# First weight slab and x loaded and rounded in alternating halves, constants queued later, six projection pieces in banks of their own

## The reference

```python
def rms_norm(x, g):
    xf = x.astype(jnp.float32)
    y = xf * lax.rsqrt(jnp.mean(xf * xf, axis=-1, keepdims=True) + EPS) * g.astype(jnp.float32)
...
def parallel_mixer(h, w_in, ...):
    proj = h @ w_in
    qk_m, v_m, o_m, i_pre, f_pre, qkv_s = jnp.split(proj, PROJ_SPLITS, axis=-1)
    qk_m = jax.nn.silu(causal_depthwise_conv(qk_m, conv_w, conv_b))
...
x = x + parallel_mixer(rms_norm(x, mix_norm_g[l]), w_in[l], ...)
```

## Time and profile before

| what | value |
|---|---|
| median of 3 runs | 1740.88 us (1739.35 to 1741.17) |
| the profiled execution, its own time | 1739.95 us |
| its span in the profile | 1738.1 us |
| PE busy | 1566.5 us, 90% of the span |
| DVE busy | 1213.2 us, 70% |
| ACT busy | 850.8 us, 49% |
| POOL busy | 364.6 us, 21% |
| mean DMA rate | 242 GB/s |

### The profile page before, as it was taken

One profiled execution on the slowest core, in us unless ns is written; L12 is line 12 of the kernel. 1 busy time (PEld: TensorE's weight loads), 2 busy tenths in 40 slices (PEclk: granted clock), 3 DMA queues, 4 the chain that ended last, 5 costly groups with the idle time before them and its releaser, 6 DMA issues.

```text
span 1738.1 us, 23835 instructions
## 1 busy us (share of the span) xinstructions
PE 1566.5 (90%) x9202; PEld 1186.1 (68%) x9202; DVE 1213.2 (70%) x2403; ACT 850.8 (49%) x1713; POOL 364.6 (21%) x326
## 2 busy tenths in 40 slices
PE   7999988789887777878888999999999999999999
PEld 6899988555532223222232588989999977689999
DVE  5697756778788888554664589666775548777764
ACT  5658734444445454333443563245554436565542
POOL 1010102445354445434443003101000200010000
PEclk9999999899999999999999999999999999899999
DMA  7333433899999999999999242123444622035544
GB/s 270 122 121 124 168 146 122 358 382 423 427 425 426 427 426 426 427 427 427 427 427 427 98 146 79 44 97 146 170 172 151 209 99 97 23 124 186 180 164 150
DMA packets 63592, 421.13 MB, mean 242 GB/s; under 512 B 8180, under 2 KB 11512, under 8 KB 15608
## 3 DMA queue, kind: packets, MB, share of 16 engines
q0 software_dynamic: 36864, 268.45, 36.7%
q1 hardware_dynamic: 23952, 148.70, 23.9%
q10 hardware_dynamic: 2664, 2.47, 0.4%
HBM read 418.54 MB, written 1.05 MB: 241 GB/s over the span
## 4 chain that ended last, share of the span: by engine, by line
PE 62%; DMA 19%; DVE 11%; ACT 6%; issue 2%; SPq 0%; POOL 0%; ACTq 0%; DVEq 0%
PE bank L377 61%; DMA uv<-in_uv,idx 18%; DVE lows L440 3%; DVE uv L1410 2%; ACT dg L389 2%; ACT acts L389 1%; ACT wp L385 1%; DMA slabs<-in_w_in 1%; PE bank L382 1%; ACT L389 1%; ACT L390 0%; DVE cacc L393 0%; ACT wf L385 0%; DVE rsb L541 0%; DVE t L720 0%
## 5 line engine op out<-in xcount | busy, mean ns | idle before, releaser
L377 PE MATMUL bank<-uv,dg 128*128 128x512 f32 x1024 | 493.0, 616 | 106.5 <-ACT dg L389 103.8
L377 PEld LDWEIGHTS bank<-uv,dg 128*128 128x128 f32 x1024 | 180.8, 191 | 407.7 <-ACT dg L389 250.4
L1410 DVE CUSTOM_DVE_ANT_0 uv<-uv,htok 128x1024 f32<-128x1024 f32 x256 | 313.1, 1224 | 169.6 <-DMA uv<-in_uv,idx 167.6
L1524 POOL DMA_INDIRECT uv<-in_uv,idx x256 | 288.2, 1126 | 373.5 <-PE bank L377 323.7
L377 PE MATMUL bank<-hn,lows 128*128 128x272 f32 (+2 forms) x704 | 200.9, 285 | 0.0
L440 DVE TENSOR_TENSOR lows<-slabs,wp 128x2048 fp32r<-128x2048 f32 (+1 forms) x78 | 167.7, 2150 | 44.6 <-ACT wp L385 44.2
L389 ACT ACTIVATE acts<-acts 128x1 f32<-128x1 f32 x256 | 51.3, 200 | 281.2 <-DVE acts L1410 280.8
L385 ACT ACTIVATE wp<-slabs 128x2048 fp32r<-128x2048 f32 (+1 forms) x78 | 140.7, 1804 | 84.3 <-DMA slabs<-in_dn 30.1
L555 POOL TENSOR_TENSOR sqT<-sqT 128x256 f32<-128x256 f32 (+1 forms) x42 | 44.8, 1066 | 621.8 <-ACT sqT L389 619.6
L440 DVE TENSOR_TENSOR lows<-slabs,whl 128x2048 fp32r<-128x2048 f32 (+1 forms) x52 | 108.3, 2082 | 39.4 <-ACT whl L385 39.3
L377 PE MATMUL bank<-hh,lows 128*128 128x272 f32 x448 | 133.1, 297 | 0.0
(11 more groups left out here) (380 smaller groups left out, 2984.0 us busy)
## 6 DMA issues: line engine op xcount, KB each, us to landing
slabs<-in_up SPq DMA_DIRECT2D x44, 1024.0 KB, 4.8
slabs<-in_w_in SPq DMA_DIRECT2D x28, 1024.0 KB, 5.1
slabs<-in_dn SPq DMA_DIRECT2D x32, 704.0 KB, 4.2
slabs<-in_wkv SPq DMA_DIRECT2D x8, 1024.0 KB, 4.8
slabs<-in_w_out SPq DMA_DIRECT2D x8, 1024.0 KB, 4.8
slabs<-in_pq SPq DMA_DIRECT2D x8, 1024.0 KB, 5.4
slabs<-in_wq SPq DMA_DIRECT2D x4, 1024.0 KB, 5.1
slabs<-in_wo SPq DMA_DIRECT2D x4, 1024.0 KB, 4.8
```

What stands on the lines that cost most here:

```text
L377: ins = T.e.matmul(pr[2] if len(pr) > 2 else out, pr[0], pr[1], start=(start and k == 0), stop=(stop and k == len(pairs) - 1), skip_group_ ...
L1410: V.e.tensor_tensor_reduce(u_, u_, htok[:, n, :], 1.0, 0.0, ALU.mult, ALU.add, acts[:, n, e_:e_ + 1]).then_inc(*V.up("dot", q))
L1524: G.e.indirect_dma_start(uv[q % NU][:, :], None, d["uv"][:, :], bass.IndirectOffsetOnAxis(ap=idx[:, n, e_:e_ + 1], axis=0)).then_inc(s_uv[ ...
```

## The change

Slab 0 and x are each loaded in two halves, in turn: half of slab 0, half of x, the other half of slab 0, the other half of x. ScalarE and VectorE split them in the same turn. ScalarE then splits slab 1 before it squares x, and slab 2 before the root. The large rest of `con`, the gates of the second layer, the memory and the meta tokens are loaded by SP behind slab 3; the last two were issued by ScalarE. The matrix of ones moves into the head of `con`, which grows from 257 to 385 columns. The pieces `w_in 1.0` and `w_in 1.1` get banks 4 and 5 instead of 0 and 1, with nothing to wait for, and `w_in 5.0`, `w_in 5.1` take 0 and 1.

```diff
-HEAD = 257
+HEAD = 385
...
+        def split_half_scalar(i):
+            hs = slice(1024 * i, 1024 * i + 1024)
+            A.wait_ge(*(loaded(0) if i else (s_first, 16)))
+            copyA(high(0)[:, hs], slab(0)[:, hs]).then_inc(*A.up("whi", 0, i))
+
+        def split_half_vector(i):
+            hs = slice(1024 * i, 1024 * i + 1024)
+            V.wait_ge(*A.at("whi", 0, i))
+            V.e.tensor_tensor(low(0)[:, hs], slab(0)[:, hs], high(0)[:, hs].bitcast(F32), ALU.subtract).then_inc(*V.up("wlo", 0, i))
...
-        PBANK[PJ[4]], PBANK[PJ[5]] = (0, PJ[0]), (1, PJ[1])
+        PBANK[PJ[4]], PBANK[PJ[5]] = (4, None), (5, None)
+        PBANK[PJ[6]], PBANK[PJ[7]] = (0, PJ[0]), (1, PJ[1])
...
         def mix1_sync():
-            load_slabs(0, 1)
             for i in range(2):
+                hs = slice(1024 * i, 1024 * i + 1024)
+                S.e.dma_start(slab(0)[:, hs], d["w_in"][0, :, hs]).then_inc(s_slab[0] if i else s_first, 16)
                 S.e.dma_start(XR[:, 4 * i:4 * i + 4, :], d["xT"][512 * i:512 * i + 512, :].rearrange("(c p) t -> p c t", p=P)).then_inc(s_x[i], 16)
-            load_slabs(1, 2)
-            S.e.dma_start(con[:, HEAD:NCON], d["con"][:, HEAD:NCON]).then_inc(s_in, 16)
+            load_slabs(1, 3)
             S.e.dma_start(gates1[:, :, :], d["gates1"][:, :, :]).then_inc(s_in, 16)
-            S.e.dma_start(gates2[:, :, :], d["gates2"][:, :, :]).then_inc(s_in, 16)
-            load_slabs(2, N_ALL)
+            load_slabs(3, 4)
+            S.e.dma_start(con[:, HEAD:NCON], d["con"][:, HEAD:NCON]).then_inc(s_con, 16)
+            S.e.dma_start(gates2[:, :, :], d["gates2"][:, :, :]).then_inc(s_con, 16)
+            S.e.dma_start(memT[:, :, :], d["memT"].rearrange("(c p) t -> p c t", p=P)).then_inc(s_mem, 16)
+            S.e.dma_start(xT[:, :, 0:16], d["metaT"].rearrange("(c p) t -> p c t", p=P)).then_inc(s_meta, 16)
+            load_slabs(4, N_ALL)
...
+            def first_ready(c):
+                T.wait_ge(*V.at("wlo", 0, c // 4))
+                h1_ready(c)
...
             for j in range(2):
-                proj("w_in", 0, j, H1, T1, h1_ready)
+                project("w_in", 0, j, pbank("w_in", 0, j)[:, 0:T1], H1, T1, first_ready)
...
-            T.wait_ge(s_in, 48)
             columns_tensor("n1", TB, B[2])
...
             V.stage("mix1")
-            split_vector(0)
             V.wait_ge(s_gain, 16)
-            for c in range(NC):
-                gain_vector("n1", XR, "mix_g", T1, H1, c)
-            ahead(PLACE["w_in", 0], split_vector)
-            V.wait_ge(s_in, 48)
+            for i in range(2):
+                split_half_vector(i)
+                for c in range(4 * i, 4 * i + 4):
+                    gain_vector("n1", XR, "mix_g", T1, H1, c)
+            split_vector(1)
+            split_vector(2)
+            V.wait_ge(s_in, 16)
...
-            split_scalar(0)
-            A.wait_ge(s_gain, 16)
-            for c in range(NC):
-                A.wait_ge(s_x[c // 4], 16)
-                gain_scalar("n1", XR, "mix_g", T1, H1[0], c)
-            A.e.dma_start(memT[:, :, :], d["memT"].rearrange("(c p) t -> p c t", p=P)).then_inc(s_mem, 16)
-            A.e.dma_start(xT[:, :, 0:16], d["metaT"].rearrange("(c p) t -> p c t", p=P)).then_inc(s_meta, 16)
+            for i in range(2):
+                split_half_scalar(i)
+                A.wait_ge(s_gain, 16)
+                A.wait_ge(s_x[i], 16)
+                for c in range(4 * i, 4 * i + 4):
+                    gain_scalar("n1", XR, "mix_g", T1, H1[0], c)
+            split_scalar(1)
             for c in range(NC):
                 square_scalar("n1", XR, T1, c)
-            ahead(PLACE["w_in", 0], split_scalar)
+            split_scalar(2)
             A.wait_ge(s_head, 16)
             root_scalar("n1", T1, B[2])
```

More of the change, by code:

```diff
@@ L33 @@
        ("ib", 1), ("fb", 1), ("alog", 1), ("dtb", 1)]
-CON = [("ident", 128), ("o1024", 128), ("eps", 1), ("o128", 128), ("bd64", 128), ("ltri", 128), ("ones", 128),
+CON = [("ident", 128), ("o1024", 128), ("eps", 1), ("ones", 128), ("o128", 128), ("bd64", 128), ("ltri", 128),
        ("nmi", 384), ("nms", 384), ("iota", 16), ("sel", 512), ("lvl", 7 * 128), ("mb1", 272), ("mb0", 144),
@@ L350, in build @@
                     selb = sbuf(ph, "selb", [4, 2 * P])
-        s_head, s_gain, s_vec, s_in = sem("con_head_loaded"), sem("first_gains_loaded"), sem("vec_loaded"), sem("con_loaded")
+        s_head, s_gain, s_vec, s_in = sem("con_head_loaded"), sem("first_gains_loaded"), sem("vec_loaded"), sem("gates1_loaded")
+        s_con, s_first = sem("con_loaded"), sem("first_half_loaded")
         s_x = [sem(f"x{i}_loaded") for i in range(2)]
@@ L636, in mix1_tensor @@
             T.wait_ge(*V.at("mrow"))
+            T.wait_ge(s_con, 32)
             for x in MIX:
@@ L670, in mlstm_tensor @@
                     T.wait_ge(*V.at("n1", "col"))
+                if h == 1:
+                    T.wait_ge(*V.at("ev", "w_in", 1, 1))
                 if h == 2:
@@ L937, in mix1_vector @@
             V.wait_ge(*V.now())
+            V.wait_ge(s_con, 32)
             V.e.tensor_tensor_scan(Bc, one1, lf, 0.0, ALU.mult, ALU.subtract).then_inc(*V.up("Bc"))
```

## The result

| | before | after |
|---|---|---|
| median of 7 runs each | 1740.88 us (1739.35 to 1744.91) | 1748.41 us (1742.88 to 1750.16) |
| ratio after / before | | 1.0032 (95%: 1.0020 to 1.0045) |
| the profiled execution | 1739.95 us, span 1738.1 | 1750.16 us, span 1748.4 |

The change makes the kernel slower, by 3.5 to 7.8 us by the interval of the ratio. Twelve later runs of it, beside 27 of the kernel before, gave 1.0017 (1.0002 to 1.0032), or 0.3 to 5.6 us (told under "A faster version").

What follows compares the result with a forecast made beforehand. Bound: the start chain up to TensorE's columns and w_in 1.0. GpSimd's chain +1.9 us and the clock about +0.9 give +2.8 on 1739.95, 1742.7; the median adds 0.9, giving 1743.6, range 1739.5 to 1747.

Steps and rivals of the forecast that it cites:

- The point that decides: TensorE's start of columns and w_in 1.0, 26.78 and 27.28 us before; any shift there carries to the end one to one.
- The squares behind slab 1's split, GpSimd late, TensorE waiting before the sum: ScalarE's squares start at 14.25 instead of 11.53, the sum at 24.4 instead of 21.57; columns possible +1.9 us.
- Two blocked additions: GpSimd's additions 1 and 4 wait for VectorE's subtractions of slabs 1 and 2; all seven end at 24.4, unblocked 21.1.
- The landing of slab 1: DMA of slab 1 lands at 12.35, 0.15 us later than before, for the 64 KB that HEAD adds.
- The clock: TensorE idles 19.4 to 24.4, then runs at low clock for 3.5 to 5.6 us; about +0.9 us more.
- The rest: Banks, constants, memory and later slabs cost nothing, lying beside TensorE's 19.29 us; a late slab would add its lateness.
- bring nothing: Bank change for w_in 1.0 gains nothing: its old wait for bank 0 was over when the columns were.
- within 0.2%: Whole time differs by less than about 3.5 us, so counted as the same; chance 0.61.

Runs made afterwards that it cites:

- A faster version: Kernel before, whole slabs, with constants behind slab 3, six banks, and TensorE's order w_in 4.0, 4.1, sum, w_in 1.0, 1.1, columns; ratio 0.9976 to before.
- delay of TensorE alone: Kernel before with 35 extra matmuls (4.1 us, results unused) on TensorE between the columns and w_in 1.0; ratio 1.0020 to the kernel before.
- no second block: Changed kernel, but VectorE subtracts slab 2 only when GpSimd's seven additions are done; ratio 0.9999 to the kernel before.
- the two fast versions: Whole slabs, six banks, late constants, columns behind w_in 1.1, against kernel before: 0.9976; same with slab 2's subtraction behind the additions, sum between w_in 4 pieces: 0.9979.
- squares first: Changed kernel with ScalarE's eight squares back ahead of the split of slab 1; ratio 1.0001 to the kernel before.
- sum late: Changed kernel with TensorE's order w_in 4.0, w_in 4.1, sum, w_in 1.0, w_in 1.1, columns; ratio 0.9992 to the kernel before.
- constants alone: Kernel before with only the change's other transfers: constants, second gates, memory, meta tokens behind slab 3, ones in the head; ratio 0.9991 to before.
- No halves: Changed kernel, but slab 0 loaded and split whole, x still in two parts; ratio 1.0006 to the kernel before.
- squares in two: Changed kernel, TensorE doing both w_in 4 pieces before the sum, ScalarE squaring chunks 0 to 3 before the gains of 4 to 7; ratio 0.9996 to before.

## Why the prediction was right, and where it was off

- *The point that decides.* Right. The delay of TensorE alone made the kernel slower by 1.0 to 6.1 us for a shift of 4.0, and "no second block" carried its 1.8 us to the end of the trace. In every version the interval of the ratio holds the shift at the mark, but it leaves out "no change" only for the changed kernel, the delay and the two fast versions.
- *The squares behind slab 1's split, GpSimd late, TensorE waiting before the sum.* Right, shown by "squares first" (3.0 of 4.05 us back) and "sum late" (the wait filled, 4.75 us back). Predicted: squares 14.25, additions 9.3 us long, end 24.4, wait 5.0. Measured: 15.58, 9.26, 25.70, 4.69.
- *Two blocked additions.* Right in place and size; one of them taken away was worth 1.87 us. (The end of the subtraction of slab 2 was put at 21.2; from 18.65 the prediction's own terms give 21.0, a slip of 0.2 us.) The Trainium skill ("SBUF — State Buffer", section "SBUF: two separate sides") says that of GpSimd and a VectorE operation with two inputs from SBUF, whichever starts first keeps the shared ports for its whole instruction, and the other waits. The traces agree: every addition that began inside a subtraction of slab 1 or 2 ended 0.6 us behind it, and a subtraction that began in an addition took 2.83 us in "constants alone"; one pair is told apart in the last section.
- *The landing of slab 1, the term that was mis-sized.* "It lands at 12.2 plus 0.15": measured 13.74. I had taken half a slab for half the time. The first half landed near 5.4, only 0.3 us before the whole slab had, not 1.2, and the first half of x at 8.1 instead of 6.7; the rate in these microseconds was about half of that before. That is +1.4 us in everything behind, and the first matmul stood at 9.31 instead of 7.8. "No halves" puts 1.1 us of it on the halves.
- *The clock.* Right in kind: 0.50 behind the wait, for 3.4 us. In size it cost less than the 0.9 us predicted: `w_in 4.1` ended at 30.8 and the reciprocal at 30.27, about 0.5 us, and 1.2 when it lasted 6.8 us.
- *The rest.* No wait for a bank, for the constants or for the memory shows: the shift of the matmuls stays at 4.1 us up to 100 us. But moving the constants back was not free, since it brought slab 2 forward into the additions ("constants alone"). And that the banks "bring nothing" holds only with TensorE's old list: with another list they are what makes the fast version possible.
- *The time.* Forecast 1743.6, +2.8; measured +5.6 by the ratio (3.5 to 7.8), +3.0 (0.3 to 5.6) the second time, and +4.1 to +5.0 at the mark. By the ratio the changed kernel takes 1746.5 us, half a microsecond inside the range that ended at 1747, while the median of its seven runs, 1748.41, lies outside. So the mechanism was right, but that the time fell into the range was partly luck. The chance of 0.61 for "within 0.2%" went to the wrong side in the first seven runs, and the twelve later ones, at 0.17%, do not decide it; with slab 1 1.4 us later the forecast would have been +4.2, beyond 3.5.

Beyond the start, 3 of the remaining 6 us between the two profiled executions stand at low stretches of the clock; for the other 3 the cause is open, and so is what sets the low stretches off in a given run.

## What to carry to other kernels

The first link of the chain that ended last is not a list of gains: slab 2 came 4.5 us sooner and the time did not move, because the next limit, the place of the sum on TensorE's list, was 0.8 us behind, and a third chain, GpSimd's additions, got 2 us slower by the very work that was now early. Before moving a block ahead on one engine, follow what stood behind it: here eight squares, 2.5 us together, fed seven additions of 8 us in all. And where TensorE waits for a small result, put independent pieces in front of that wait; free banks are what makes this possible.

## What the runs showed of the hardware that I had not expected

Halving a transfer did not halve its time to land: 512 KB of slab took 4.7 us from its issue where 1 MB, issued at the same time, had landed within 5.0 (0.75 to 5.74). From 3 to 5 us the halves and the other first transfers moved at 194 and 252 GB/s; with the whole slab it was 411 and 412 in the kernel before, and 378 and 419 in "no halves". And the contention of VectorE and GpSimd goes both ways: a subtraction of 2.29 us took 2.83, and a product of 0.22 took 0.76, when an addition was under way. In "squares in two" an addition that is recorded 0.01 us ahead of a subtraction (18.38 and 18.39) was the one that waited: it took 2.90 us, and the subtraction its usual 2.29.
